# A two-layer hybrid decoder trunk: x kept with tokens on partitions, and activations held in place for the down, output and conv projections

## The reference, cut to what matters

```python
for l in range(2):
    x = x + 0.5 * swiglu(rmsnorm(x, norm_ffn1_g[l]), ffn1_w_gate[l], ffn1_w_up[l], ffn1_w_down[l])
    h = rmsnorm(x, norm_mix_g[l])
    proj = h @ w_in[l]
    q, k, v, c_b, c_c, c_u, g_attn, g_conv = split(proj)     # 512 x 6, 1024 x 2
    attn = rmsnorm(diff_attention(q, k, v, rel_bias, lam), subln_g[l]) * (1 - lambda_init)
    y_attn = attn @ w_branch_attn[l]
    y_conv = (c_b * causal_depthwise_conv(c_c * c_u, conv_w[l])) @ w_branch_conv[l]
    merged = sigmoid(g_attn) * y_attn + sigmoid(g_conv) * y_conv
    x = x + merged @ w_out[l]
    x = x + 0.5 * swiglu(rmsnorm(x, norm_ffn2_g[l]), ffn2_w_gate[l], ffn2_w_up[l], ffn2_w_down[l])
return rmsnorm(x, final_g)
```

## Time and profile before

| | us |
|---|---|
| median of 3 runs | 1071.25 (1071.04 to 1072.55) |
| span of the profiled execution | 1069.1 |
| PE busy | 1061.2 (99%) |
| DVE busy | 748.7 (70%) |
| ACT busy | 596.7 (56%) |
| POOL busy | 190.7 (18%) |
| TensorE clock granted, mean | 0.999 of full speed |

### The profile page before, as it was taken

How to read it: one execution, slowest core, us unless ns; L and a number is a source line. 1 busy time by engine, 2 the same in 40 slices (tenths; PEclk the granted TensorE clock), 3 DMA queues, 4 the chain that set the end, 5 groups by cost and what they waited for, 6 DMA issues and landing times.

```text
span 1069.1 us, 16546 instructions
## 1 busy us (share of the span) xinstructions
PE 1061.2 (99%) x5380; PEld 901.1 (84%) x5380; DVE 748.7 (70%) x950; ACT 596.7 (56%) x859; POOL 190.7 (18%) x347
## 2 busy tenths in 40 slices
PE   9999999999999999999999999999999999999997
PEld 7888888888889888888888888888888988888886
DVE  6766657868788866665776666668787887676654
ACT  7555445555775755444555544445657666455463
POOL 0354320000250022230002223000004400222300
PEclk9999999999999999999999999999999999999999
DMA  7888886655796687875668787566558967878862
GB/s 243 261 262 243 244 266 200 204 167 162 219 318 200 203 248 243 244 235 189 198 206 250 242 243 225 179 216 190 149 165 258 292 221 223 251 241 253 272 235 79
DMA packets 205223, 238.92 MB, mean 223 GB/s; under 512 B 17940, under 2 KB 179520, under 8 KB 205040
## 3 DMA queue, kind: packets, MB, share of 16 engines
q1 hardware_dynamic: 189968, 198.82, 59.6%
q0 software_dynamic: 14800, 38.86, 12.1%
q10 hardware_dynamic: 400, 0.51, 0.1%
HBM read 218.46 MB, written 19.67 MB: 223 GB/s over the span
## 4 chain that ended last, share of the span: by engine, by line
PE 98%; DMA 0%; ACT 0%; SPq 0%; DVE 0%; issue 0%; DVEq 0%
PE acc L1658 21%; PE acc L1639 17%; PE acc L1640 17%; PE acc L1641 17%; PE acc L1667 11%; PE acc L1734 2%; PE acc L1736 2%; PE acc L1737 2%; PE acc L1662 1%; PE acc L1857 1%; PE mixed L1662 1%; PE score L1662 1%; PE acc L1858 1%; PE acc L1859 1%; PE acc L1615 1%; DMA raw<-in_ffn_w_up_dram 0%
## 5 line engine op out<-in xcount | busy, mean ns | idle before, releaser
L1083 DVE TENSOR_TENSOR w_lo<-raw,w_hi 128x1024 fp32r<-128x1024 f32 x382 | 455.4, 1205 | 224.9 <-ACT w_hi L678 224.0
L678 ACT CAST w_hi<-raw 128x1024 fp32r<-128x1024 f32 (+1 forms) x381 | 390.8, 1037 | 307.8 <-PE acc L1641 201.1
L1639 PE MATMUL acc<-w_hi,xm 128*128 128x512 f32 x816 | 319.2, 391 | 0.0
L1641 PE MATMUL acc<-w_lo,xm 128*128 128x512 f32 x816 | 317.8, 390 | 0.0
L1640 PE MATMUL acc<-w_hi,xm 128*128 128x512 f32 x816 | 317.8, 389 | 0.0
L1658 PE MATMUL acc<-hm,w_hi 128*128 128x512 f32 x656 | 206.2, 396 | 0.0
L1641 PEld LDWEIGHTS acc<-w_lo,xm 128*128 128x128 f32 x816 | 153.2, 188 | 32.0
L1639 PEld LDWEIGHTS acc<-w_hi,xm 128*128 128x128 f32 x816 | 153.2, 188 | 31.8 <-issue 0.2
L1640 PEld LDWEIGHTS acc<-w_hi,xm 128*128 128x128 f32 x816 | 153.3, 188 | 31.3
L1667 PEld LDWEIGHTS acc<-hm,w_lo 128*128 128x128 f32 x720 | 133.3, 188 | 29.0
L540 POOL DMA_DIRECT2D hid_scratch<-sum x176 | 96.3, 554 | 341.5 <-DVE sum L1185 339.7
(11 more groups left out here) (192 smaller groups left out, 884.1 us busy)
## 6 DMA issues: line engine op xcount, KB each, us to landing
raw<-in_ffn_w_gate_dram SPq DMA_DIRECT2D x176, 256.0 KB, 3.1
raw<-in_ffn_w_up_dram SPq DMA_DIRECT2D x176, 256.0 KB, 3.7
raw<-in_ffn_w_down_dram SPq DMA_DIRECT2D x164, 256.0 KB, 3.5
raw<-in_w_in_dram SPq DMA_DIRECT2D x160, 256.0 KB, 3.4
hid_scratch<-sum POOLq DMA_DIRECT2D x176, 64.0 KB, 3.1
part<-hid_scratch POOLq DMA_DIRECT2D x44, 256.0 KB, 3.6
raw<-in_w_out_dram SPq DMA_DIRECT2D x32, 256.0 KB, 3.8
gate_scratch<-acc_lo POOLq DMA_DIRECT2D x64, 64.0 KB, 3.3
```

The source lines that it names most:

```text
L678: nc.scalar.copy(w_hi[:, s, 0:tiles, :], raw[:, s, 0:tiles, :]).then_inc(hi_split, 1)
L1083: nc.vector.tensor_tensor(w_lo[:, s, 0:tiles, :], raw[:, s, 0:tiles, :], w_hi[:, s, 0:tiles, :], ALU.subtract).then_inc(lo_split, 1)
L1639: nc.tensor.matmul(s[:, t, :], xh, wh[:, k], start=not u and not k, stop=False, skip_group_check=True)
L1641: mm = nc.tensor.matmul(s[:, t, :], xh, wl[:, k], start=False, stop=(u, k) == (GU_UNITS - 1, GK - 1), skip_group_check=True)
```

## The change

1. **Down, output and conv projections by token.** Down (the three that were not yet), output projection and the 12 conv units run with activations in place. The conv results then have tokens on partitions, so they are block-transposed by DVE and shuffled through DRAM by POOL like the gates (`shuffle_set`).
2. **x with tokens on partitions** (`x_tok`). DVE adds half of the columns at a time (`new_x`), PE transposes the new x, 8 blocks of 128 x 128 at a time (`turn_x`), into two PSUM banks, and ACT and DVE make `xm` from there (`rounded_x`, `remainder_x`). This is done twice before each of five stages: mixer 1, FFN2 of layer 1, FFN1 of layer 2, mixer 2, FFN2 of layer 2. The first half (`turn_x(0)`) sits two units into the second half of a down or output projection, the second half (`turn_x(1)`) two units into the next stage.
3. **Norms from row sums.** ACT squares x with a running sum over its row; `mean_square` on PE, the sums of squares on DVE and `to_tokens` go. Where q and k need the factor along the columns, one matmul (`rstd_rows` with `mean_ones`) spreads it, once in each layer.
4. **Order of units.** The next stage starts with work on the first half of x. In gate and up two sets are interleaved (`SET_STARTS`). In the mixer two q sets start together, then `turn_x(1)`, two v units, the rest of q, the spreading matmul, and so on; v goes to the `score` banks instead of `acc`.
5. The turning back of x for the last stage (DVE transposes, DRAM trip, ACT copies) goes.

The core of the diff (a line of "..." marks what is left out):

```diff
+            def turn_x(c):
+
+                adds.add(QT)
+                wait(pe, (x_new, adds.now))
+                for p in (2 * c, 2 * c + 1):
+                    for k in range(PAIR):
+                        kt = p * PAIR + k
+                        for t in range(QT):
+                            col = (k * QT + t) * P
+                            mm = nc.tensor.transpose(turned_x[p % 2][:, col:col + P], x_tok[:, t, kt * P:(kt + 1) * P],
+                                                     ident[:, :])
+                    mm.then_inc(x_turned, 1)
...
+            def next_gate_up():
+
+                banks = [new_set(), None]
+                for i, u in SET_STARTS:
+                    if (i, u) == (1, 0):
+                        turn_x(1)
+                        banks[1] = new_set()
+                    gate_up_unit(banks[i], u)
...
+                        if c and u == 1 and not last:
+                            turn_x(0)
...
             for l in range(DEPTH):
                 ffn(l == 0)
-                normed_sets(V_ITER)
...
+                banks = [new_set(), new_set()]
+
+                def quarter(j, n):
+                    multiply(banks[j], [xm[:, n * UK + k, :] for k in range(UK)], n == 0, n == 1,
+                             (xm_lo, pairs.now - (1 - n) * UK // PAIR))
+
+                quarter(0, 0)
+                quarter(1, 0)
+                turn_x(1)
+                gate_up_unit(score, 0)
+                gate_up_unit(score, 1)
+                quarter(0, 1)
+                quarter(1, 1)
+                wait(pe, (rstd_masked, l + 1))
+                nc.tensor.matmul(rstd_ps, mean_ones[:, :], rstd_rows[:, :, :].rearrange("p t n -> p (t n)"), start=True,
+                                 stop=True).then_inc(rstd_spread, 1)
+                banks[0] = new_set()
+                quarter(0, 0)
+                quarter(0, 1)
+                gate_up_unit(score, 2)
+                gate_up_unit(score, 3)
+                banks[1] = new_set()
+                quarter(1, 0)
+                quarter(1, 1)
...
-                for i in range(OUT_ITERS):
-                    two_sets(merged, merged_lo, branch_pairs, in_turn=i == 0)
+                for c in range(2):
+                    s = new_set()
+                    for u in range(OUT_UNITS):
+                        gate_up_unit(s, u, merged, merged_lo, branch_pairs)
+                        if c and u == 1:
+                            turn_x(0)
...
+            def new_x(c, factor, units):
+
+                bank = acc[sets.fixed % ACCS]
+                sets.add()
+                adds.add(QT)
+                wait(dve, (used, units))
+                for t in range(QT):
+                    x_at = x_tok[:, t, cols_of(c)]
+                    nc.vector.scalar_tensor_tensor(out=x_at, in0=bank[:, t, :], scalar=factor, in1=x_at, op0=ALU.mult,
+                                                   op1=ALU.add).then_inc(x_new, 1)
+                wait(dve, (x_new, adds.now))
+                dve.sem_inc(acc_summed, 1)
...
+            def next_units(factor, gains):
+
+                new_x(1, factor, split.now - LEAD + RING)
+                lo()
+                lo()
+                mean_squares()
+                lo()
+                remainder_x(1, gains)
+                lo()
+                lo()
+                norm_rstd()
```

More of the change, by code:

```diff
@@ L660, in _ @@
             sets = Count()
[L661 removed]
+            turns = Count(XPAIRS)
+            adds = Count()
             norm = Count()
@@ new lines, in remainder_x @@
+            def remainder_x(c, gains):
+                for p in (2 * c, 2 * c + 1):
+                    pair.add()
+                    wait(dve, (xm_hi, pair.now))
+                    for k in range(PAIR):
+                        kt = p * PAIR + k
+                        last = nc.vector.scalar_tensor_tensor(
+                            out=xm[:, kt, SEQ:2 * SEQ], in0=turned_x[p % 2][:, k * SEQ:(k + 1) * SEQ],
+                            scalar=cur[:, gains + kt:gains + kt + 1], in1=xm[:, kt, 0:SEQ].bitcast(F32),
+                            op0=ALU.mult, op1=ALU.subtract)
+                    last.then_inc(xm_lo, 1)
@@ L1334, in ffn @@
                 hid_of_set(0)
-                lo(down_tiles(LEAD))
-                remainder((GU_ITERS - 2) * PAIR, 1)
+                if last:
+                    last_down()
+                    return
                 if first:
@@ L1486, in taps @@
                     own(last)
-                turn_gates()
+                turn_set()
                 lo()
-                nc.vector.tensor_tensor(conv_in, conv_in, conv, ALU.mult).then_inc(conv_in_ready, 1)
+                wait(dve, (conv_back[1], 16 * layers.now), (conv_back[2], 16 * layers.now))
+                for j in range(2):
+                    last = nc.vector.tensor_tensor(
+                        in_quarters(conv_in[:, j * PAIR:(j + 1) * PAIR, :]), set_by_channel(conv_raw[1])[:, j],
+                        set_by_channel(conv_raw[2])[:, j], ALU.mult)
+                last.then_inc(conv_in_ready, 1)
                 lo()
@@ L1513, in _ @@
                 lo()
-                turn_gates()
-                nc.vector.tensor_tensor(conv, conv, conv_b, ALU.mult).then_inc(conv_ready, 1)
+                turn_set()
+                wait(dve, (conv_back[0], 16 * layers.now))
+                for j in range(2):
+                    c_at = in_quarters(conv[:, j * PAIR:(j + 1) * PAIR, :])
+                    last = nc.vector.tensor_tensor(c_at, c_at, set_by_channel(conv_raw[0])[:, j], ALU.mult)
+                last.then_inc(conv_ready, 1)
                 lo()
```

809 lines of the change are left out of this document (315 added, 494 removed).

## The result

The changed kernel took **1075.2 us** in the median of seven runs (1073.9 to 1076.19); the kernel before, run beside it, took 1071.99 us (1071.01 to 1072.55). The ratio is **1.0028**, 95% interval 1.0018 to 1.0039: slower by about 3 us. The forecast was 1074.5 us with a range of 1071.0 to 1078.5.

What follows compares the result with a forecast made beforehand. PE, busy 99% of the span, was taken to bound the kernel. Turns 9.1, mixer wait 3.3 and tight wait 0.4 less savings 9.5 gave +3.3 us on 1071.25, forecast 1074.5 us, range 1071.0 to 1078.5.

Steps and rivals of the forecast that it cites:

- The bound: Whole kernel: PE is busy 99% of the span, so its matmul starts set the time and no wait can be won.
- Down, 4.4 us: Three down stages by token: 59.8 us instead of 61.3 each, saving 4.4 us in all.
- Output projection 1.1 us: Output projection by token: 21.8 us instead of 22.30, saving 0.54 us in each layer, 1.1 us in all.
- norms 1.8 us: Norms: six matmuls with 1/1024 go and two spreading matmuls come, 0.45 us each, saving 1.8 us.
- Conv columns, 2.2 us: Heads 0 to 2 save 0.26 us each, v and first conv unit 0.4 after 0.1 for switching; 2.2 us in all.
- Turns, 9.1 us: Ten turns of eight PE transposes of x, about 0.91 us each with start-up, add 9.1 us.
- The mixer's wait, 3.3 us: Ahead of each mixer's first unit PE waits for the second accumulator until DVE's additions end, T + 1.65; adds 3.3 us.
- the rival "no change": The wait in the mixer costs nothing and the rest cancels, giving 1071.3 us; chance 0.2.
- The tight wait, 0.4 us: Mixer: third q set needs the first's accumulator, about 3.2 us against 2.79 + 0.24 of other work; adds 0.4 us in two layers.
- Costed at nothing: Rounding and remainder of new x, the conv sets' shuffle (12.6 us under about 16) and the last stage's x cost nothing.
- The rival of the second wait: Late conv shuffle in the heads makes PE wait some 5 us in a layer, 1084.5 us; chance 0.06.
- The sum: Whole kernel: 9.1 + 3.3 + 0.4 - 9.5 = +3.3 us, forecast 1074.5 us, 0.3% slower; chance 0.64.

Runs made afterwards that it cites:

- the first experiment: Changed kernel, but in the mixer the second accumulator is asked for only after the first q unit, first v unit and the turn; 1072.0 us, ratio 1.0000.

## Why the prediction was right

**The bound.** PE at 99%: right. The time followed PE's starts in every run, and the 57 us that DVE lost were worth nothing. That there was no wait to win was not quite so: one of 0.18 us stood in each mixer, shows it as 14.11 busy of 14.13, and the change took it away unforeseen.

**Down, 4.4 us.** Right: 60.73 us with a turn of 0.89 is 59.84, against the 59.8 forecast. In the first layer 0.17 us is missing (35.54 us for thirteen units instead of 35.36, behind one small matmul at the change of stage).

**Output projection 1.1 us and norms 1.8 us.** FFN1 of layer 1 lost 0.57 us with its norm matmul. From the gate columns to the end of FFN2 the changed kernel is 0.83 us longer with two turns in it (1.78), so it saved 0.95 there, against 0.54 + 0.45 = 0.99 forecast. Over the four FFN stages the norms gave about 2.0 us.

**Conv columns, 2.2 us.** The size is near, the reason was partly wrong. The heads gave 0.6 us a layer and not 0.78. The 0.4 us of the stretch of v came, but 0.3 of it was PE's wait for an accumulator, which the prediction took for slower units and a price of 0.1 for switching; it went because v left the accumulators. The conv columns alone gave 1.4.

**Turns, 9.1 us.** Right: 0.79 us for eight, and two units behind one take 5.54 instead of 5.44, so 0.89 and not 0.91. Its two rows did not both give 0.91: the eight with their start-up give 0.79 + 0.09 = 0.88, the three at their pace give 0.64 + 0.12 = 0.76. In the changed kernel:

```profile
166.03 1.03 PE L1613 MATMUL mixed<-ident,x_tok 128*128 128x128 f32 x8
...
166.82 0.48 PE L1651 MATMUL acc<-w_hi,hm 128*128 128x512 f32 x1
167.13 0.40 PE L1653 MATMUL acc<-w_hi,hm 128*128 128x512 f32 x1
167.37 0.39 PE L1654 MATMUL acc<-w_lo,hm 128*128 128x512 f32 x1
```

The Trainium skill (TensorE: Matmul & The Clock Gate, Part 4: PE-mode transpose) has some 275 ns for one transpose; the records here are again 272 ns long, and doubling the turns shows what counts in a stream, 0.11 us. Taken as the distance between starts, its figure would, as an estimate, put the doubled kernel 22 us over the changed one; 8.6 were measured. Its statement that transposes don't count as busy finds nothing to show itself in here: the clock stays at 1.00 behind eight and behind sixteen.

**The mixer's wait, 3.3 us.** Right: T + 1.65 forecast, T + 1.64 in the trace, and the first experiment removed it. The last 0.15 us of the chain, the signal, had no row behind it, so that it fitted to 0.01 us is in part luck. Not foreseen was the start-up of 0.09 us behind the pause. It decided the sign. Without it the change is worth nothing either way, which is where the rival "no change" put it by denying the wait.

**The tight wait, 0.4 us.** The mechanism and the length of the pause were right: the chain of about 3.2 us against a cover of 3.03 gives 0.17 in each layer, and 0.43 - 0.24 = 0.19 is in the trace. DVE's sum of the first set, which ends it:

```profile
210.28 0.68 DVE L1061 TENSOR_TENSOR by_token_at<-acc,acc_lo 128x512 f32<-128x512 f32 x1
```

It ends at 210.96 and PE goes on at 211.02. Mis-sized was what such a pause costs: with it the start-up behind the spreading matmul is 0.07 us shorter, so 0.24 us in all and not 0.4.

**Costed at nothing.** The rounding of the new x, the conv sets' trip and the last stage: PE waits for no other engine elsewhere after the start-up, so all three covers held. That of the conv sets held by less than forecast: the last one of layer 1 is turned at 267.34, its return is issued at 274.39 and such returns land 6.7 us later in the median, 13.8 us and not 12.6, against a cover of about 16. The rival of the second wait did not happen; with the change POOL is busy 16.29 us in the heads of layer 1 instead of 1.20, under full cover.

**The sum.** In the body: turns 8.9, waits 3.3 + 0.2, start-up behind the mixer's waits 0.2, savings 4.2 (down), 1.1 (output), 2.0 (conv and v) and 2.0 (norms), together +3.3, as the traces differ. The prediction's +3.3 is as close only because its errors cancel: turns 0.2 and the tight wait 0.2 too high, down 0.2 and conv 0.2 too high on the other side, norms 0.2 too low, the start-up missing. What the prediction did not have at all is the start-up of the kernel: it compared with one span of before, 1069.1 us, which was an early start, and the same kernel gave 1070.1 later.

## What to carry to other kernels

When PE has no idle time, check for each accumulator when PE asks for it again against when its reader is done with it: the end of the last matmul plus the reader's two additions and a hand-over gave this wait, and asking for the accumulator two units and a turn later removed it. Look for such waits on the weight loads too, since PE's overlapping records hide pauses under 0.16 us and most of one of 0.18. Work that is cheap on a full engine is still paid in full: three turns moved back to DVE and the DMA queues, where a stage of 24 us hides them, brought 2.6 us. For differences of 0.1% to 0.3%, compare the traces from the first steady unit on, since the start-up alone moves by more.

## What the runs showed of the hardware

- The start-up, up to the first by-token unit, took 19.70, 20.21 and 20.79 us in three profiles of one kernel, and 21.34 and 20.40 in two of the other; the rest of the span repeated within 0.1 us out of 1050.
- A transpose of 128 x 128 in the stream costs 0.099 us in eights and 0.11 us for each of eight more, with a record of 272 ns.
- Behind a small matmul the next ones start late, 0.31 and 0.24 us apart instead of 0.227. A pause has such a start-up too, 0.09 us behind the 1.64 us of the mixer. Where both meet they don't add up: taking 0.19 us of pause away behind the spreading matmul gained only 0.12.
- A change between weights in place and activations in place costs almost nothing, 0.23 and 0.24 us from start to start. The 0.41 us found near it was a wait for DVE's sum.
- From the end of DVE's last addition to PE's start it took 0.16 us at the mixer's wait and 0.06 us at each of the two short ones.
- By an estimate from its spans, the kernel with both waits gone started up at least 0.8 us earlier than its neighbours on two chips. No cause was found.
